# GpSimd takes 22 low parts of the MLP, the projection another bank order, and the tile parts another place

## The reference, cut to what matters

```python
m = rms_norm(h, mlp_norm[i])
h = h + jnp.square(jax.nn.relu(m @ w_mlp_up[i])) @ w_mlp_down[i]
gate = jax.nn.sigmoid(rms_norm(h, ple_norm[i]) @ w_ple_gate[i] + b_ple_gate[i])
h = h + (p[i] @ w_ple_proj[i]) * gate
```

## Time and profile before

| What | Value |
|---|---|
| Median of three executions | 1637.92 us (1636.62 to 1639.0) |
| Profiled execution, its own time | 1636.67 us |
| Its span, first to last instruction | 1634.7 us |
| Mean granted clock of TensorE | 0.999 |
| PE busy | 1624.7 us (99%) |
| DVE busy | 1028.6 us (63%), 1545 instructions |
| ACT busy | 660.0 us (40%) |
| POOL busy | 84.5 us (5%), 80 instructions |

### The profile page before, as it was taken

How to read it: one execution, slowest core, us unless ns; L and a number is a source line. 1 busy time by engine, 2 the same in 40 slices (tenths; PEclk the granted TensorE clock), 3 DMA queues, 4 the chain that set the end, 5 groups by cost and what they waited for, 6 DMA issues and landing times.

```text
span 1634.7 us, 20169 instructions
## 1 busy us (share of the span) xinstructions
PE 1624.7 (99%) x8480; PEld 1347.5 (82%) x8480; DVE 1028.6 (63%) x1545; ACT 660.0 (40%) x919; POOL 84.5 (5%) x80
## 2 busy tenths in 40 slices
PE   9999999999999999999999999999999999999999
PEld 7877878898989878888888888877777888888887
DVE  6797673796866847577466457545655576366353
ACT  5576435354444446433223223456565333122221
POOL 1300000000000000000000000312101100000000
PEclk9999999999999999999999999999999999999999
DMA  5310228345454521223222313322221223222311
GB/s 190 114 37 27 104 78 145 72 105 131 98 121 86 161 77 54 79 104 125 103 103 81 109 75 118 106 79 100 76 76 52 78 103 106 101 102 95 112 59 71
DMA packets 28058, 156.00 MB, mean 95 GB/s; under 512 B 3712, under 2 KB 5392, under 8 KB 12096
## 3 DMA queue, kind: packets, MB, share of 16 engines
q1 hardware_dynamic: 26352, 149.75, 25.5%
q0 software_dynamic: 1328, 4.86, 5.2%
q10 hardware_dynamic: 288, 0.10, 0.0%
HBM read 149.98 MB, written 4.72 MB: 95 GB/s over the span
## 4 chain that ended last, share of the span: by engine, by line
PE 73%; DVE 5%; ACT 2%; issue 1%; POOL 0%; DVEq 0%; ACTq 0%
PE bank L722 19%; PE bank L723 18%; PE bank L724 18%; PE bank L728 3%; PE bank L730 2%; PE bank L729 2%; PE bank L1180 2%; PE bank L1182 2%; PE bank L1181 2%; PE bank L1417 1%; PE bank L1427 1%; PE bank L1443 1%; DVE WL L1907 1%; DVE X L1937 1%; DVE WLR L2445 1%
## 5 line engine op out<-in xcount | busy, mean ns | idle before, releaser
L1907 DVE TENSOR_TENSOR WL<-RAW,WH 128x2048 fp32r<-128x2048 f32 (+2 forms) x122 | 273.1, 2243 | 176.7 <-ACT WH L1486 176.7
L722 PE MATMUL bank<-AH,WH 128*128 128x512 f32 (+1 forms) x974 | 383.1, 393 | 0.2 <-DVE X L1937 0.2
L724 PE MATMUL bank<-AH,WL 128*128 128x512 f32 (+1 forms) x974 | 379.6, 390 | 0.0
L723 PE MATMUL bank<-AL,WH 128*128 128x512 f32 (+1 forms) x974 | 379.6, 390 | 0.0
L1486 ACT ACTIVATE WH<-RAW 128x2048 fp32r<-128x2048 f32 (+2 forms) x122 | 227.0, 1867 | 172.0 <-PE bank L724 138.0
L723 PE MATMUL bank<-HL,WH 128*128 128x512 f32 x608 | 236.8, 390 | 0.0
L722 PE MATMUL bank<-HH,WH 128*128 128x512 f32 x608 | 236.8, 390 | 0.0
L724 PE MATMUL bank<-HH,WL 128*128 128x512 f32 x608 | 236.8, 389 | 0.0
L722 PEld LDWEIGHTS bank<-AH,WH 128*128 128x128 f32 (+1 forms) x974 | 182.5, 187 | 40.8 <-issue 2.4
L724 PEld LDWEIGHTS bank<-AH,WL 128*128 128x128 f32 (+1 forms) x974 | 182.6, 187 | 38.7
L723 PEld LDWEIGHTS bank<-AL,WH 128*128 128x128 f32 (+1 forms) x974 | 182.6, 187 | 38.4 <-issue 1.0
(11 more groups left out here) (346 smaller groups left out, 2375.6 us busy)
## 6 DMA issues: line engine op xcount, KB each, us to landing
RAW<-in_W SPq DMA_DIRECT2D x124, 1024.0 KB, 4.8
RAW<-in_W SPq DMA_DIRECT2D x9, 768.0 KB, 4.2
X<-in_XT SPq DMA_DIRECT2D x16, 256.0 KB, 5.2
ev_scratch<-ev POOLq DMA_DIRECT2D x16, 160.0 KB, 7.6
Gb<-ev_scratch SPq DMA_DIRECT2D x16, 128.0 KB, 3.1
Gb<-ev_scratch SPq DMA_DIRECT2D x16, 112.0 KB, 2.7
out<-X SPq DMA_DIRECT2D x7, 256.0 KB, 2.0
RAW<-in_W SPq DMA_DIRECT2D x2, 512.0 KB, 5.2
```

Of the source, the lines that this page charges most:

```text
L722: e.matmul(o, a, h, start=first, stop=False)
L723: e.matmul(o, a, l, start=False, stop=False)
L724: return e.matmul(o, c, h, start=False, stop=last)
L1907: e.tensor_tensor(k.WL[j][:, 0:n], k.RAW[RAW_OF[u]][:, 0:n], k.WH[j][:, 0:n].bitcast(F), SUB).then_inc(*WLO.mark(u))
```

## The change

- The low parts of the 22 tiles of fast units go from DVE to POOL: `pool_program` walks `mlp_order` itself and does them at step "low", with the unit's bias row issued ahead of the odd tile. Whoever waited for DVE's mark waits for POOL's (`low_is_in`).
- In `turn_order` the step "low" of the even tile moves behind the block sums' steps "mid" and "turned". On DVE that step is now empty.
- The bank counter is set to 4 before the projection, whose tiles then use banks 4, 5, 6, 0, 1, 2, 3, 4. The counter runs on from there up to the second block's attention, which sets it anew.
- In the last down group DVE writes `AH` and `AL` of a tile before it adds the square.

```diff
+def low_is_in(k, m):
+    return (k.POOL if UNIT["up", m // 2] in FAST else k.DVE)("hl", "down", m)
...
     if after and fast:
         yield "post", m
-        yield "low", m
     if fast:
         yield "mid", u
         yield "turned", u
+    if after and fast:
+        yield "low", m
...
-            w.wait_ge(DVE("hl", name, base + c))
+            w.wait_ge(DVE("hl", name, base + c) if name != "down" else low_is_in(k, base + c))
...
     u = UNIT["proj", 0]
     a, l = split_view(k, u, 2)
+    ring[0] = 4
     w.wait_ge(WLO(u), DVE("pL"))
...
         if m > 1:
-            w.wait_ge(DVE("hl", "down", m - 2))
+            w.wait_ge(low_is_in(k, m - 2))
...
-        elif step in ("rest", "low"):
+        elif step == "rest":
...
             if g == 3:
+                parts(2, PC_PLE, m, MM("up", 31))
                 if m:
                     add_square(2, m)
-                parts(2, PC_PLE, m, MM("up", 31))
...
+    def bias_row(i):
         w.wait_ge(MM("up", 2 * i))
         e.dma_start(k.EV.ap()[i:i + 1], k.ev[i:i + 1, None, :].to_broadcast([1, 64, 640])).then_inc(k.arrived["ev"], 16)
+
+    w.wait_ge(DVE("ev"))
+    for i in range(FIRST_FAST):
+        bias_row(i)
+    for step, *x in mlp_order():
+        if step == "low":
+            m, = x
+            if m % 2:
+                bias_row(m // 2)
+            w.wait_ge(ACT("hh", "down", m))
+            e.tensor_tensor(k.HL[m % NH][:, :], k.t2s[m % 2][:, :], k.HH[m % NH][:, :].bitcast(F), SUB).then_inc(*POOL.mark("hl", "down", m))
```

More of the change, by code:

```diff
@@ L1154, in first_downs @@
             s = (8 * g + c) % NH
-            w.wait_ge(DVE("hl", "down", 8 * g + c))
+            w.wait_ge(low_is_in(k, 8 * g + c))
             for m in range(2):
@@ L2713, in pool_program @@
     root(1)
-    w.wait_ge(DVE("ev"))
-    for i in range(16):
+    def bias_row(i):
         w.wait_ge(MM("up", 2 * i))
         e.dma_start(k.EV.ap()[i:i + 1], k.ev[i:i + 1, None, :].to_broadcast([1, 64, 640])).then_inc(k.arrived["ev"], 16)
+    w.wait_ge(DVE("ev"))
[8 more added lines that the diff above has]
+            e.tensor_tensor(k.HL[m % NH][:, :], k.t2s[m % 2][:, :], k.HH[m % NH][:, :].bitcast(F), SUB).then_inc(*POOL.mark("hl", "down", m))
     w.wait_ge(MM("up", 31))
@@ L2724, in pool_program @@
     root(3)
-    w.wait_ge(DVE("hl", "down", 31), ACT("usq", 31), MM("pool", 7))
+    w.wait_ge(low_is_in(k, 31), ACT("usq", 31), MM("pool", 7))
     for z in k.t1s:
```

## The result

| What | Before | After |
|---|---|---|
| Median (range, executions) | 1638.43 us (1636.62 to 1640.56, 7) | 1633.06 us (1631.21 to 1634.07, 7) |
| Ratio, 95% interval | | 0.9966 [0.9955, 0.9977] |
| Profiled execution, its own time | 1636.67 us | 1633.97 us |
| Its span | 1634.7 us | 1632.2 us |
| Mean granted clock of TensorE | 0.999 | 0.998 |

The change makes the kernel 5.4 us faster, 0.34%. The forecast was 5.6 us and 1632.3, the measured median is 1633.06. In the changed kernel the lines stand 6 or 7 further down: L722 is L728, L744 is L750, L750 is L756, L1180 is L1186, L2445 is L2452.

A forecast was written before the change was run, and what follows sets the result against it. PE's matmuls bound the kernel (busy 1624.7 of 1634.7 us), so only its waits could be won: -5.4 at the projection and -0.2 from the low parts, -5.6 in all, from 1637.92 to 1632.3 us; range 1630.2 to 1636.0.

The forecast's parts named there:

- The bank order: At the first projection matmul: PE's wait for bank 3 goes, -3.73 us, and the half clock behind it, -1.67: -5.4 us.
- DVE in the last down group: Tile 7 starts right behind its product, tiles take 3.2 us instead of 3.9, and `dg` is complete 2 us early.
- The spread, price 0: After the sum of squares: DVE's mean and diagonal come in time, 0.7 us to spare, so the spread costs nothing.
- the first rival: The wait moves to the spread, behind a weight split: price up to 1.2 to 1.3 us, 1633.6 us; chance 0.12.
- The low parts, -0.2 us: Fast units 7 and 8: with POOL doing the low parts, each of two waits shrinks by 0.1 us.
- `pe_x` 6 us later, 0: On POOL's queue: the `pe_x` load waits for the last low part, costing nothing as its use comes mid down group.
- Place of "low", the counter further on, 0: In the step list and after the projection: DVE and POOL keep their order, and the later bank numbers cost nothing.
- granted clock 1.00 throughout: Sign expected in the profile after: TensorE's granted clock at 1.00 everywhere, with no half-clock stretch.

The follow-up runs named there:

- e1_bank_only: The kernel before with the bank counter set to 4 before the projection, nothing else; 1634.63 us, ratio 0.9975.
- e9_bank_parts: The kernel before with the bank counter at 4 and `AH`/`AL` written ahead of the square's sum, low parts left on DVE; 1632.05 us, ratio 0.9961.
- e11_after_again: The changed kernel measured once more, with nothing altered, on the chip of other follow-up kernels; 1631.82 us, ratio 0.9960 against the kernel before.
- e3_pool_only: The changed kernel without its bank line and with the old order of tile parts and square: only low parts moved to POOL; 1637.15 us, ratio 0.9989.
- e2: The kernel before with `AH` and `AL` written ahead of the square's sum in the last down group, nothing else; 1635.48 us, ratio 0.9981.
- e5_pool_twice: The changed kernel with each of the 22 low parts computed twice in a row on POOL; 1634.24 us, ratio 0.9971 against the kernel before.
- e12_late_pe_early: The changed kernel with the even tile's squaring and low part behind "stageB", and `pe_x` issued ahead of the last two low parts; 1630.96 us, ratio 0.9952.

## Why the prediction was right

**The bank order, -5.4 us**: the gap shrank by 3.73 and the half clock's share by 1.68, both as the sum had them. (Banks 5, 6, 0, 1 and 2 had held tiles 1, 2, 4, 5 and 6, and not, as the prediction says, 1 to 6 without 0; nothing hangs on it.) The prediction gave the whole of it to the bank and let the tile parts only keep the next steps on time. e1_bank_only shows the bank's own part: -5.4 us up to the sum of squares, and 1.25 us given back at the spread. What the prediction did not say is that the tile parts alone get 3.3 us, since a shorter standstill spares the clock too.

**DVE in the last down group**: tile 7 was forecast to start right behind its product, and did in that profile (579.59 + 0.39 to 580.02), but 1.0 and 1.5 us later in e9_bank_parts and e11_after_again. The tiles ahead of it took 3.2 us where before they took 3.9. `dg` was complete 1.9 us ahead of the sum, forecast 2.

**The spread, price 0**: the mean was forecast 0.99 us behind the sum and came 0.98 behind; the diagonal was done at 588.25, 0.69 us ahead of the spread. Right in the profiled execution, but with no more room than that: 0.7 us late in e11_after_again, the first rival in small.

**The low parts, -0.2 us**: measured -0.45 over the fast stretch, -0.48 at the two waits themselves. The mechanism was right: "stageB" was held until POOL was done (360.61) and ended 0.55 us later, at 361.16, the distance of the earlier trace rows, while `YZ` and `G`, which read a bank, took their usual 0.42. From the start of ACT's quarter to the end of "stageB" it took 2.02 us (359.14 to 361.16), before 2.28 (355.70 to 357.98), so 0.26 us less per unit where I took 0.1. POOL needed 1.30 us where the prediction worked with 1.35 to 1.55, and so held DVE for less. The Trainium skill (GPSIMD Engine Reference, section 8) names DVE instructions with two SBUF inputs as those that contend; the runs agree, with 0.76 instead of 0.68 us for the piece that ends behind one low part, and 1.1 us more for the pair under a doubled one.

**`pe_x` 6 us later, 0**: right for the sum, incomplete as it was argued. It was issued 5.0 us later than before, counted from the start of the down group. The prediction looked at when `pe_x` is used and not at what it travels beside. In most profiles with it and the band beside them the weight loads landed 0.7 to 2 us later, and in e3_pool_only, where ACT waited for one, the gap was 0.9 us longer. A late weight unit also came without the meeting (e9_bank_parts), so how much of this is `pe_x`'s doing is open. The slack that the tile parts make hides most of it. The step to do differently is the same either way: a DMA moved in time is priced by its neighbours too.

**Place of "low", the counter further on, 0**: nothing speaks against it; past the spread all kernels measured here agree (1039.8 to 1040.0 us from there to the last matmul).

**A sign that failed**: "granted clock 1.00 throughout". The passage had it, the attention at 192 us did not. It is no work of the change, as e11_after_again, the same kernel, has 1.00 there, and kernels built on the one before have it too (e1, e2, e9).

**The total**: the medians give -5.4, forecast -5.6, with an interval from -3.8 to -7.4 us. e11_after_again gives -6.7 for the same kernel. That the total comes within 0.2 us of the forecast is luck: the stretches of the two profiles sum to 5.9, with the low parts at 0.45 where 0.2 was forecast. The sum is confirmed by its places in the profile more than by the total, which can't tell 0.5 us.

## What to carry to other kernels

Price a wait of PE with the clock behind it, and ask of each edit whether it removes the wait or shortens it to one that no half clock follows (here none followed 1.76 us, and one followed 3.22): shortening it from 3.7 to 1.8 us got 3.3 of 5.4 us, and the two edits don't add up. When a wait goes, walk to the next two things due and count their slack, here 2 us and 0.7 us. Before moving work to an idle engine, look whether another order on the engine that is waited for does the same: here ACT's order freed the units of seven, and GpSimd's 22 operations brought half a microsecond.

## What the runs showed of the hardware

- **The half clock in the attention.** In 7 of the 13 profiles besides that of the kernel before, TensorE fell to 1.2 GHz between 191.67 and 193.70 us for 3.41 or 6.83 us, without having stood idle. What it does before that are, from 187 to 192.8 us (the last 0.8 us of which lie in the half clock), small matmuls, the same in every kernel of this case; in the changed one (groups of PE, count, then busy us and mean ns of one):

```profile
L1075 PE MATMUL bank<-cst,sq 128*128 128x1 f32 x16 | 2.3, 276 | 0.0
L1057 PE MATMUL bank<-AT,gv 128*128 128x128 f32 x16 | 1.9, 275 | 0.0
L1064 PE MATMUL bank<-dd,ST 64*128 64x64 f32 x28 | 1.8, 275 | 0.0
```

It costs 1.7 or 3.4 us, as much as many a change, and comes in some executions and not in others of one kernel (6.83 us in the first profile of the changed one, none in the second). Mean clocks of 0.998 to 1.000 among the seven executions of the changed kernel go with it: 1634.07 us at 0.998, 1631.21 at 1.000. What decides it in an execution was not tried and stays open.
- **GpSimd and DVE** hold each other up: a 128x512 subtraction on POOL took 1.30 us at its shortest, and in e5_pool_twice 2.33 under DVE's pair of splits and 3.2 under its split of a whole unit; DVE's pair of 2.36 us took 3.47.
- **Two loads of 0.5 MB** from POOL's queue, both beside the weight loads: the band landed after 7.1 to 9.5 us in eight profiles, and after 3.7 or 3.8 in the five with `pe_x` at its old moment (6.4 in e12_late_pe_early). The weights' median landing was 4.9 to 7.0 us against 5.0 to 5.3, with 6.3 in one of the five, so for them the cause is not shown.
